# Retention scores from split queries and keys instead of plain fp32 ones

## The chip, the cores and the metric

The kernel runs on one core of a Trainium2 chip. The metric is the time on the device of one execution, in microseconds (us). A core has several engines that run side by side and meet through semaphores: PE (TensorE, the matmuls), DVE (VectorE), ACT (ScalarE), POOL (GpSimd) and SP (SyncE, which issues the weight transfers). PEld is PE's loading of weights, which has rows of its own in the trace.

## The reference

Two transformer blocks on 512 tokens of width 1024: forgetting attention with memory attention, then retention with memory attention, then a third layer of dilated attention, convolution and a gated feed-forward part. The change touches one place, the scores of retention (12 heads, keys of width 64, values of width 128):

```python
qf = rotary(q.reshape(B, S, H, dk).astype(jnp.float32), pos)
kf = rotary(k.reshape(B, S, H, dk).astype(jnp.float32), pos) * (dk ** -0.5)
...
inner = jnp.einsum('bhnd,bhmd->bhnm', qc, kc) * d_inner[None]
o = jnp.einsum('bhnm,bhme->bhne', inner, vc)
...
out = out * lax.rsqrt(jnp.mean(out * out, axis=-1, keepdims=True) + EPS)
```

The reference goes through the 512 tokens in chunks of 128 with a carried state. The kernel computes the same sums without the state, as four 128-row strips of a causal 512 by 512 score matrix per head, multiplied by a table of decays.

## The kernel before

Everything is held with the features on the 128 partitions and the 512 tokens along the free axis. A projection `products(...)` is 8 chunks of 128 input features times three matmuls of 128 by 128 by 512: weights and activations are each a high part in the rounded format fp32r and a low part (the rest), and high times high, high times low and low times high are summed in a PSUM bank (lines 2208 to 2210). One weight block after another goes this way: SP loads it (`wraw`), ACT rounds it (`whi`, line 766), POOL makes the rest (`wlo`, line 611), PE uses it. Each engine runs its own program in the order in which it is written, and all the waits are written out by hand.

Retention is the phase "ret": six turns i = 0 to 5, two heads in each (e = 0 and 1). The two heads of a turn share a tile of 128 partitions: head e has its 64 features in rows 64e to 64e + 63 of `q` and `k`. In a turn PE does, in this order: the projection of the queries (with the two heads' means of the turn before in its middle, lines 2484 and 2485), of the keys, of the first gate, then `ret_scores(i)`, then the projection of the second gate, then `ret_values` and `ret_values_low` (line 2463), which weigh the values.

`ret_scores` writes scores in eight matmuls, one for each head and strip j, with (e, j) in the order (0,0) (1,0) (0,2) (1,1) (0,1) (1,3) (0,3) (1,2). Strip j has 512 - 128j columns, so each head has 512 + 384 + 256 + 128 = 1280 columns. `q` and `k` are plain fp32 tiles here. The matmuls of the two heads use different halves of the rows of the PE array. They write to A0 to A3 and to PV, and PV is shared: strip 2 of head 0 stands in its first half, strip 2 of head 1 in its second. Before the last matmul, (1,2), PE therefore waits on the semaphore `r_half`, which (0,2) raises.

The scores' operands come from `rope` (lines 1710, 1711 and 1714), which runs once for the queries and once for the keys: ACT copies the projection with its 32-row groups swapped into the bank VT (`ret_swap`, line 960, four copies), DVE multiplies the projection by the cosines into `q` or `k`, multiplies VT by the sines, and adds the two. VT serves both, so ACT's swap for the keys waits on `r_roped` until DVE has added the queries. On DVE the queries' rotation of turn i stands behind the end of turn i - 1, that is `ret_low`, `ret_gate` and `ret_out` (lines 1688 to 1702) for the two heads of that turn, which in turn needs the squares and the roots from ACT and the means from PE. Behind the rotation of the keys DVE takes the first gate out of PSUM (`z[0]`, line 1728), then multiplies the scores by the decays (line 1681).

Of the kernel before, what the change touches and what calls it, by code (L numbers as in the profile page):

```python
# [7 lines left out]
F32 = mybir.dt.float32  # L8
F32R = mybir.dt.float32r
BF16 = mybir.dt.bfloat16  # L10
ALU = mybir.AluOpType
# [3 lines left out]
P = 128  # L15
S = 512
# [5 lines left out]
HEADS = 12  # L22
# [6 lines left out]
DK = P // 2  # L29
# [89 lines left out]
def build(nc, t, out):  # L119
# [3 lines left out]
    with ctx:  # L123
        def sb(name, shape, dt=F32, scope=ctx):
            return scope.enter_context(nc.sbuf_tensor(name, shape, dt))
# [4 lines left out]
        def sem(name):  # L130
            return ctx.enter_context(nc.semaphore(name))
# [41 lines left out]
        with ExitStack() as one:  # L173
            Oh = sb("Oh", [P, INNER // P, S], F32R, one)
            Ol = sb("Ol", [P, INNER // P, S], F32R, one)
            Mh = sb("Mh", [P, KC, NMEM], F32R, one)
            Ml = sb("Ml", [P, KC, NMEM], F32R, one)
            with ExitStack() as memory:
                qm_high, qm_low = (sb(f"qm_{part}", [P, S], F32R, memory) for part in ("high", "low"))
            q = sb("q", [P, S], F32, one)  # L180
            k = sb("k", [P, S], F32, one)
            vm_low0 = sb("vm_low0", [P, S], F32R, one)
            with ExitStack() as squared:
                r_high = [sb(f"r_high{e}", [P, S], F32R, squared) for e in range(2)]
# [23 lines left out]
            with ExitStack() as squared:  # L208
                r_low = [sb(f"r_low{e}", [P, S], F32R, squared) for e in range(2)]
# [12 lines left out]
        osq, decayed = (sq2, sq), (probsT, probs)  # L222
        decayed_high = [x[:, HEADS:HEADS + 4, :].rearrange("p c n -> p (c n)")[:, 0:1280] for x in (Oh, Ol)]
        decayed_low = (probs_high[:], turned_low[:])
        maskf, acc2 = sq2[:, 0:P], z[0]

        q_high, k_high, q_low = r_high[0], r_high[1], r_low[1]
# [55 lines left out]
        swapped = VT[:]  # L283
# [65 lines left out]
        r_half = sem("r_half")  # L349
        r_low_made = sem("r_low_made")  # L350
        r_swap, r_roped, r_tanh, r_table = (sem(x) for x in ("r_swap", "r_roped", "r_tanh", "r_table"))
# [20 lines left out]
        def since(eng, s, value):  # L372

            if not isinstance(value, int) or value > 0:
                eng.wait_ge(s, value)
# [99 lines left out]
        def ret_place(e, j):  # L475

            bank, at = ((A[e], 0), (A[2 + e], 0), (PV, 2 * P * e), (A[2 + e], 3 * P))[j]
            return bank[:, at:at + S - j * P]
# [14 lines left out]
        def weighed(r):  # L493

            return 4 * (r // 2) + r % 2 + 1

        def squared(r):

            return weighed(r) + 2

        def split_values(group, j):

            at = slice(4 * group, 4 * group + 4), slice(j * P, (j + 1) * P)
            return Oh[:, at[0], at[1]], Ol[:, at[0], at[1]]
# [914 lines left out]
        def _(dve):  # L1419
            own = Own(dve, dve_own)  # L1420
            tt, ts, stt = dve.tensor_tensor, dve.tensor_scalar, dve.scalar_tensor_tensor
# [5 lines left out]
            def arrived(name, i, b):  # L1427

                dve.wait_ge(w_used, PH[name].n(i, b) + 1)
# [266 lines left out]
            def ret_low(r, e):  # L1696
                dve.wait_ge(r_high_made, squared(r))
                tt(r_low[e][:], osq[e][:], r_high[e][:].bitcast(F32), ALU.subtract).then_inc(r_low_made, 1)
# [5 lines left out]
            def rope(i, b, dst):  # L1704

                ph = PH["ret"]
                arrived("ret", i, b)

                dve.wait_ge(r_swap, i * 2 + (b + 1))
                tt(dst[:], proj[ph.bank(b)][:], rcos[:], ALU.mult).then_inc(evac, 1)  # L1710
                own.mark(tt(swapped, swapped, rsin[:], ALU.mult))
                own.settle()
                dve.wait_ge(evac, ph.g(i, b) + 1)
                tt(dst[:], dst[:], swapped, ALU.add).then_inc(r_roped, 1)

            def ret_turn(i):
                ph = PH["ret"]
                if i:
                    ret_low(i * 2 - 2, 0)
                    ret_low(i * 2 - 1, 1)  # L1720
                    ret_gate(i - 1, 1)
                    ret_out(i * 2 - 2, 0)
                    ret_out(i * 2 - 1, 1)
                rope(i, 0, q)
                rope(i, 1, k)
                arrived("ret", i, 2)
                since(dve, r_table, i * 2 - 1)
                tt(z[0][:], proj[ph.bank(2)][:], rms[:], ALU.mult).then_inc(evac, 1)
                ret_decay(i * 2, 0, i)
                ret_decay(i * 2 + 1, 1, i)  # L1730
                for r in (i * 2, i * 2 + 1):
                    dve.wait_ge(r_high_made, weighed(r))
                    tt(decayed_low[r % 2], decayed[r % 2][:], decayed_high[r % 2].bitcast(F32), ALU.subtract).then_inc(r_low_made, 1)
                ret_gate(i, 0)
                arrived("ret", i, 3)
                since(dve, r_table, i * 2)
                tt(z[1][:], proj[ph.bank(3)][:], rms[:], ALU.mult).then_inc(evac, 1)
# [336 lines left out]
            for c in range(KC - 1):  # L2074
                i, b = divmod(c, 2)
# [102 lines left out]
            for i in range(NT):  # L2178
                for h in range(2):
                    y, at = y_bank[i][h][:], slice(h * S, (h + 1) * S)  # L2180
# [4 lines left out]
                for h in range(2):  # L2185
                    y, at = y_bank[i][h][:], slice(h * S, (h + 1) * S)
# [3 lines left out]
        def _(pe):  # L2190
            mm = pe.matmul
# [254 lines left out]

            def ret_scores(i):

                pe.wait_ge(r_roped, i * 2 + 2)
                since(pe, r_decayed, i * 2)  # L2450
                since(pe, r_out, i * 2)
                for e, j in ((0, 0), (1, 0), (0, 2), (1, 1), (0, 1), (1, 3), (0, 3), (1, 2)):
                    rows = slice(DK * e, DK * e + DK)
                    if (e, j) == (1, 2):
                        pe.wait_ge(r_half, i + 1)
                    ins = mm(ret_place(e, j), k[rows, j * P:(j + 1) * P], q[rows, j * P:S], start=True, stop=True)  # L2456
                    if (e, j) == (0, 2):
                        ins.then_inc(r_half, 1)
                ins.then_inc(r_scores, 1)

            def ret_weigh(e, j, x, y, start=False, stop=False):

                return mm(ret_sum[e][:, j * P:S], x, y[:, TRI[j]:TRI[j] + S - j * P], start=start, stop=stop)  # L2463
# [9 lines left out]

            def ret_values_low(r, e):

                pe.wait_ge(r_low_made, weighed(r))
                for j in range(NT):
                    ins = ret_weigh(e, j, Oh[:, r, j * P:(j + 1) * P], decayed_low[e], stop=(j == NT - 1))
                ins.then_inc(r_pv, 1)

            def ret_mean(r, e):

                pe.wait_ge(r_low_made, squared(r))
                mm(A[2 + e][:], mean_r[:], r_high[e][:], start=True, stop=False)
                mm(A[2 + e][:], mean_r[:], r_low[e][:], start=False, stop=True).then_inc(r_ms, 1)

            def ret_means(i):
                return lambda c: (ret_mean(i * 2, 0), ret_mean(i * 2 + 1, 1)) if c == 4 else None

            def ret_turn(i):  # L2490
                products("ret", i, 0, 0, H, each=ret_means(i - 1) if i else None)
                products("ret", i, 1, 1, H)
                products("ret", i, 2, 2, H)
                pe.wait_ge(v_low, R_VALUE_LOW + HEADS)
                ret_scores(i)
                products("ret", i, 3, 3, H)
                ret_values(i * 2, 0)
                ret_values(i * 2 + 1, 1)
                ret_values_low(i * 2, 0)
                ret_values_low(i * 2 + 1, 1)  # L2500
# [80 lines left out]
            for b in range(HEADS):  # L2581
# [8 lines left out]
                if b == 1:  # L2590
                    pe.wait_ge(rms_ready, 2)
                    for i in range(NT):
                        ins = mm(VT[:, i:i + 1], rms[:, i * P:(i + 1) * P], mean_d[:, 0:1], start=True, stop=True)
# [161 lines left out]
            for b, c in ((0, 0), (0, 1), (0, 2), (1, 0), (1, 1), (1, 2), *((b, c) for c in range(3, KC) for b in range(2))):  # L2755
# [6 lines left out]
                ins = mm(bank[:], wlo[at][:, c, :], Gh[:, c, :], start=False, stop=(c == KC - 1))  # L2762
# [11 lines left out]
            for h in range(2):  # L2774
                y, of = last_out[h][:, 0:HALF], slice(h * HALF, (h + 1) * HALF)
                for c in range(KC):
# [8 lines left out]
                    ins = mm(y, wlo[at][:, c, :], Gh[:, c, of], start=False, stop=(c == KC - 1))  # L2785
# [68 lines left out]
            for c in range(KC):  # L2854
# [5 lines left out]
                ins = mm(A[3][:], wlo[fourth][:, c, :], Hh[:, c, :], start=False, stop=(c == KC - 1))  # L2860
# [38 lines left out]
            def down_part(f, i, h):  # L2899

                s = dn.slot(f // 2 % 2, f % 2)
                y, at, w = y_bank[i][h][:], slice(i * P, (i + 1) * P), slice(4 * h, 4 * h + 4)
                high, low = (x[s][:, w, :].rearrange("p c n -> p (c n)") for x in (whi, wlo))
                mm(y, Fh[:, f, at], high, start=(f == 0), stop=False)  # L2904
                mm(y, Fl[:, f, at], high, start=False, stop=False)  # L2905
                return mm(y, Fh[:, f, at], low, start=False, stop=(f == FC - 1))  # L2906
# [12 lines left out]
            for i, h in tiles:  # L2919
# [8 lines left out]
                for f in range(2):  # L2928
                    ins = down_part(f, i, h)
                    if (i, h) == tiles[-1]:  # L2930
                        ins.then_inc(w_used, 1)
            for f in range(2, FC - 3):
                down_ready(f)
                for i, h in tiles:
                    ins = down_part(f, i, h)
# [71 lines left out]
```

## Time and profile before

| | us |
|---|---|
| median of 3 runs | 1815.93 (1815.48 to 1816.66) |
| the profiled execution, its whole time | 1815.78 |
| its span (first to last instruction) | 1814.1 |
| PE busy | 1806.9 (100% of the span) |
| DVE busy | 942.2 (52%) |
| ACT busy | 773.1 (43%) |
| POOL busy | 789.3 (44%) |

The granted clock of PE was 0.999 of full speed over the span. Rows of the timeline give the start of an instruction and its duration. PE's matmuls are pipelined: a row lasts until its result is complete, and the next one starts before that, so what a matmul costs PE is read from start to start. An fp32 matmul stands in the trace as two rows, each over all of its columns.

### The profile page before, as it was taken

What the parts mean: (1) busy time and instruction counts of PE and PEld (TensorE: products, weight loads), DVE (VectorE), ACT (ScalarE), POOL (GpSimd) and SP (SyncE); (2) the same over time, 40 slices, a digit from 0 to 9 for tenths busy, and PEclk for the clock granted to TensorE, in tenths of its full rate; (3) what the DMA queues carried; (4) which work ended last, traced back from release to release, by engine and by line L of the source; (5) the groups of instructions that cost most, each with busy time, mean ns of one, the idle gap of its engine ahead of it and who ended that gap; (6) DMA issues with size and microseconds to landing.
All of it is one profiled execution on the core that took longest, in us unless ns stands there. A gap on an engine that the chain in (4) does not pass through costs nothing.

```text
span 1814.1 us, 23727 instructions
## 1 busy us (share of the span) xinstructions
PE 1806.9 (100%) x8577; PEld 1506.6 (83%) x8577; DVE 942.2 (52%) x1607; ACT 773.1 (43%) x1240; POOL 789.3 (44%) x380
## 2 busy tenths in 40 slices
PE   9999999999999999999999999999999999999998
PEld 7888888888888888888888888888888888888887
DVE  6246556554111666654259989956333564544202
ACT  5344444443333666643343233257323474444213
POOL 3444444444444333444444543353444454444442
PEclk9999999999999999999999999999999999999999
DMA  5333333333333323332333433322333333333332
GB/s 176 100 93 82 93 82 88 111 87 105 92 93 109 100 81 93 105 93 88 98 93 93 113 88 90 75 82 70 95 102 93 93 94 93 94 103 104 96 101 93
DMA packets 285751, 173.99 MB, mean 96 GB/s; under 512 B 14800, under 2 KB 271208, under 8 KB 285664
## 3 DMA queue, kind: packets, MB, share of 16 engines
q1 hardware_dynamic: 275264, 164.70, 31.7%
q0 software_dynamic: 2496, 8.07, 1.6%
q10 hardware_dynamic: 7904, 0.06, 0.2%
q8 instruction: 55, 0.90, 0.2%
q14 instruction: 32, 0.26, 0.0%
HBM read 170.62 MB, written 2.19 MB: 95 GB/s over the span
## 4 chain that ended last, share of the span: by engine, by line
PE 99%; DVE 0%; ACT 0%; issue 0%; DVEq 0%; ACTq 0%
PE proj L2208 23%; PE proj L2210 23%; PE proj L2209 23%; PE A L2541 1%; PE A L2543 1%; PE A L2542 1%; PE A L2904 1%; PE A L2905 1%; PE A L2906 1%; PE A L2366 1%; PE A L2463 1%; PE PV L2463 1%; PE proj L2543 1%; PE proj L2542 1%; PE proj L2541 1%; PE A L2456 1%
## 5 line engine op out<-in xcount | busy, mean ns | idle before, releaser
L611 POOL TENSOR_TENSOR wlo<-wraw,whi 128x1024 fp32r<-128x1024 f32 (+1 forms) x304 | 723.8, 2385 | 918.4 <-ACT whi L766 914.2
L766 ACT ACTIVATE whi<-wraw 128x1024 fp32r<-128x1024 f32 (+1 forms) x303 | 317.5, 1049 | 613.4 <-DMA wraw<-w_in 168.4
L2208 PE MATMUL proj<-Hh,whi 128*128 128x512 f32 x1424 | 562.5, 395 | 0.0
L2210 PE MATMUL proj<-Hh,wlo 128*128 128x512 f32 x1424 | 555.1, 390 | 0.0
L2209 PE MATMUL proj<-Hl,whi 128*128 128x512 f32 x1424 | 554.7, 390 | 0.0
L2210 PEld LDWEIGHTS proj<-Hh,wlo 128*128 128x128 f32 x1424 | 267.3, 188 | 56.3
L2208 PEld LDWEIGHTS proj<-Hh,whi 128*128 128x128 f32 x1424 | 267.5, 188 | 55.1 <-issue 0.7
L2209 PEld LDWEIGHTS proj<-Hl,whi 128*128 128x128 f32 x1424 | 267.6, 188 | 54.0 <-issue 0.7
L1835 DVE SCALAR_TENSOR_TENSOR A<-cin,dwT,A 128x512 f32<-128x512 f32 x232 | 175.1, 755 | 6.8
L2208 PE MATMUL proj<-Oh,whi 128*128 128x512 f32 x256 | 99.8, 390 | 0.0
L2209 PE MATMUL proj<-Ol,whi 128*128 128x512 f32 x256 | 99.6, 389 | 0.0
L2210 PE MATMUL proj<-Oh,wlo 128*128 128x512 f32 x256 | 99.6, 389 | 0.0
L1748 DVE TENSOR_TENSOR X<-X,proj 128x512 f32 (+1 forms) x16 | 11.0, 687 | 93.9 <-PE proj L2210 93.9
L2144 DVE TENSOR_TENSOR uv<-proj,rms 128x512 f32<-128x512 f32 x21 | 14.5, 692 | 81.2 <-PE proj L2210 81.2
L2210 PEld LDWEIGHTS proj<-Oh,wlo 128*128 128x128 f32 x256 | 48.1, 188 | 9.9
L2209 PEld LDWEIGHTS proj<-Ol,whi 128*128 128x128 f32 x256 | 48.1, 188 | 9.9
L2208 PEld LDWEIGHTS proj<-Oh,whi 128*128 128x128 f32 x256 | 48.1, 188 | 9.8
L2182 DVE TENSOR_TENSOR VT<-VT,gains 128x512 f32<-128x512 f32 x1 | 0.7, 699 | 101.4 <-ACT sq L1408 101.4
L869 ACT ACTIVATE ztanh<-z 128x512 f32<-128x512 f32 x20 | 12.7, 633 | 72.3 <-DVE z L1625 43.2
L2007 DVE TENSOR_TENSOR sq<-proj,rms 128x512 f32<-128x512 f32 x16 | 11.0, 691 | 54.6 <-PE proj L2210 54.3
L1580 DVE RECIPROCAL small<-small 128x4 f32<-128x4 f32 x20 | 3.6, 178 | 67.1 <-ACT probs L840 67.1
L1599 DVE SCALAR_TENSOR_TENSOR ob<-PV,gate 128x512 f32<-128x512 f32 x20 | 13.8, 691 | 47.2 <-PE PV L2389 25.8
(561 smaller groups left out, 3045.2 us busy)
## 6 DMA issues: line engine op xcount, KB each, us to landing
wraw<-w_in SPq DMA_DIRECT2D x68, 512.0 KB, 3.9
wraw<-fox_w_in SPq DMA_DIRECT2D x56, 512.0 KB, 3.8
wraw<-ret_w_in SPq DMA_DIRECT2D x44, 512.0 KB, 3.8
wraw<-w_up SPq DMA_DIRECT2D x44, 512.0 KB, 3.9
wraw<-w_out SPq DMA_DIRECT2D x40, 512.0 KB, 4.1
wraw<-w_down SPq DMA_DIRECT2D x22, 512.0 KB, 3.5
wraw<-w_mem_kv SPq DMA_DIRECT2D x16, 512.0 KB, 3.9
wraw<-conv_pw_w SPq DMA_DIRECT2D x8, 512.0 KB, 4.1
```

Of the source, the lines that this page charges most:

```text
L611: pool.tensor_tensor(wlo[s][:, 0:r, :], wraw[s][:, 0:r, :], whi[s][:, 0:r, :].bitcast(F32), ALU.subtract).then_inc(w_lo, 1)
L766: f(whi[s][:, 0:r, :], wraw[s][:, 0:r, :], ACT.Copy).then_inc(w_hi, 1)
L1835: ins = stt(conv_sum if tap < CONV - 1 else C[:, c, :], cin[:, c, tap:tap + S], dwT[:, c * CONV + tap:c * CONV + tap + 1], conv_sum, ALU.m ...
L2208: mm(dst, whi[s][:, c, :], xh, start=(first and c == 0), stop=False)
L2209: mm(dst, whi[s][:, c, :], xl, start=False, stop=False)
L2210: ins = mm(dst, wlo[s][:, c, :], xh, start=False, stop=(last and c == chunks - 1))
L2366: ins = pe.transpose(A[j][:, (i - j) * P:(i - j + 1) * P], probs[:, FOXAT[i] + j * P:FOXAT[i] + (j + 1) * P], ident[:])
L2456: ins = mm(ret_place(e, j), k[rows, j * P:(j + 1) * P], q[rows, j * P:S], start=True, stop=True)
L2463: return mm(ret_sum[e][:, j * P:S], x, y[:, TRI[j]:TRI[j] + S - j * P], start=start, stop=stop)
L2541: mm(y, Hh[:, x, at], high[:, c, :], start=(x == 0), stop=False)
L2542: mm(y, Hl[:, x, at], high[:, c, :], start=False, stop=False)
L2543: ins = mm(y, Hh[:, x, at], low[:, c, :], start=False, stop=(x == KC - 1))
```

## The change

DVE now makes two tiles from each rotated tile: the rounded high part (written straight from the addition, in format fp32r) and the low part, which is the fp32 sum less the high part. They are put where there is room: the high parts into chunk 15 of `Oh` (queries) and of `Ol` (keys), the low parts into `qm_high` (queries) and `qm_low` (keys). The scores are then key-high times query-high, key-high times query-low and key-low times query-high, each in the eight matmuls of before, accumulated in the same banks. The semaphore `r_low_made`, which counted four steps of a turn, counts seven, and `r_half` is raised five times in a turn.

```diff
+                high, low = roped_high[b], roped_low[b]
+                if b == 0:
+                    own.mark(tt(high, dst[:], swapped, ALU.add))
+                else:
+                    tt(high, dst[:], swapped, ALU.add).then_inc(r_low_made, 1)
                 tt(dst[:], dst[:], swapped, ALU.add).then_inc(r_roped, 1)
+                if b == 0:
+                    own.settle()
+                else:
+                    dve.wait_ge(r_low_made, k_high_count(i))
+                dve.wait_ge(r_roped, i * 2 + (b + 1))
+                tt(low, dst[:], high.bitcast(F32), ALU.subtract).then_inc(r_low_made, 1)
...
-                pe.wait_ge(r_roped, i * 2 + 2)
+                pe.wait_ge(r_low_made, k_high_count(i))
...
-                for e, j in ((0, 0), (1, 0), (0, 2), (1, 1), (0, 1), (1, 3), (0, 3), (1, 2)):
-                    rows = slice(DK * e, DK * e + DK)
-                    if (e, j) == (1, 2):
-                        pe.wait_ge(r_half, i + 1)
-                    ins = mm(ret_place(e, j), k[rows, j * P:(j + 1) * P], q[rows, j * P:S], start=True, stop=True)
-                    if (e, j) == (0, 2):
-                        ins.then_inc(r_half, 1)
+                for n, (x, y) in enumerate(((roped_high[1], roped_high[0]), (roped_high[1], roped_low[0]), (roped_low[1], roped_high[0]))):
+                    if n == 2:
+                        pe.wait_ge(r_low_made, k_low_count(i))
+                    for e, j in ((0, 0), (1, 0), (0, 2), (1, 1), (0, 1), (1, 3), (0, 3), (1, 2)):
+                        rows = slice(DK * e, DK * e + DK)
+                        if (e, j) == (1, 2):
+                            pe.wait_ge(r_half, 5 * i + 2 * n + 1)
+                        if (e, j) == (0, 2) and n:
+                            pe.wait_ge(r_half, 5 * i + 2 * n)
+                        first = n == 0 and (e, j) in ((0, 0), (1, 0), (0, 2), (1, 1), (0, 1))
+                        ins = mm(ret_place(e, j), x[rows, j * P:(j + 1) * P], y[rows, j * P:S], start=first, stop=(n == 2 and (e, j) in ((0, 0), (1, 0), (0, 3), (1, 3), (1, 2))))
+                        if (e, j) == (0, 2) or (e, j) == (1, 2) and n < 2:
+                            ins.then_inc(r_half, 1)
```

PE at the scores of turn 1, before (the names are the banks, then the two operands; what the instruction waits on stands in brackets):

```order
L2456 MATMUL A0<-q,k 128x512 [waits r_decayed,r_out,r_roped,v_low]
L2456 MATMUL A1<-q,k 128x512
L2456 MATMUL PV<-q,k 128x256
L2456 MATMUL A3<-q,k 128x384
L2456 MATMUL A2<-q,k 128x384
L2456 MATMUL A3<-q,k 128x128
L2456 MATMUL A2<-q,k 128x128
L2456 MATMUL PV<-q,k 128x256 [waits r_half]
L2208 MATMUL proj1<-Hh,whi3 128x512 [waits w_lo,evac]
```

The same place in the change, the first product and the start of the second (`Ol` holds the keys' high part, `Oh` and `qm_high` the queries' high and low part):

```order
L2494 MATMUL A0<-Oh,Ol 128x512 [waits r_decayed,r_out,r_low_made,v_low]
L2494 MATMUL A1<-Oh,Ol 128x512
L2494 MATMUL PV<-Oh,Ol 128x256
L2494 MATMUL A3<-Oh,Ol 128x384
L2494 MATMUL A2<-Oh,Ol 128x384
L2494 MATMUL A3<-Oh,Ol 128x128
L2494 MATMUL A2<-Oh,Ol 128x128
L2494 MATMUL PV<-Oh,Ol 128x256 [waits r_half]
L2494 MATMUL A0<-qm_high,Ol 128x512
L2494 MATMUL A1<-qm_high,Ol 128x512
L2494 MATMUL PV<-qm_high,Ol 128x256 [waits r_half]
```

Eight matmuls have become 24, and the waits on `r_half` five instead of one: before each second use of PV, in either direction.

DVE at the rotations of turn 1, before:

```order
L1710 TENSOR_TENSOR q<-proj0,rcos 128x512 [waits r_swap,w_used]
L1711 TENSOR_TENSOR VT<-VT,rsin 128x512
L1714 TENSOR_TENSOR q<-q,VT 128x512 [waits evac,dve_own]
L1710 TENSOR_TENSOR k<-proj1,rcos 128x512 [waits r_swap,w_used]
L1711 TENSOR_TENSOR VT<-VT,rsin 128x512
L1714 TENSOR_TENSOR k<-k,VT 128x512 [waits evac,dve_own]
L1728 TENSOR_TENSOR z0<-proj0,rms 128x512 [waits r_table,w_used]
```

And in the change:

```order
L1731 TENSOR_TENSOR q<-proj0,rcos 128x512 [waits r_swap,w_used]
L1732 TENSOR_TENSOR VT<-VT,rsin 128x512
L1737 TENSOR_TENSOR Oh<-q,VT 128x512 [waits evac,dve_own]
L1740 TENSOR_TENSOR q<-q,VT 128x512
L1746 TENSOR_TENSOR qm_high<-q,Oh 128x512 [waits r_roped,dve_own]
L1731 TENSOR_TENSOR k<-proj1,rcos 128x512 [waits r_swap,w_used]
L1732 TENSOR_TENSOR VT<-VT,rsin 128x512
L1739 TENSOR_TENSOR Ol<-k,VT 128x512 [waits evac,dve_own]
L1740 TENSOR_TENSOR k<-k,VT 128x512
L1746 TENSOR_TENSOR qm_low<-k,Ol 128x512 [waits r_roped,r_low_made]
L1760 TENSOR_TENSOR z0<-proj0,rms 128x512 [waits r_table,w_used]
```

The queries' high part stands ahead of the addition that raises `r_roped`, and its low part behind it; `z0` and the decays behind it stand two more instructions down.

## Rows read from the trace of the kernel before

**Rows 1.** The page: busy time of the engines, and the chain that ended last.

```profile
PE 1806.9 (100%) x8577; PEld 1506.6 (83%) x8577; DVE 942.2 (52%) x1607; ACT 773.1 (43%) x1240; POOL 789.3 (44%) x380
PE 99%; DVE 0%; ACT 0%; issue 0%; DVEq 0%; ACTq 0%
```

**Rows 2.** Busy time by window, from scores to scores (first and last of five).

```profile
592.55:621.63 29.08, 29.08 (x141) 23.93 (x140) 20.10 (x30) 19.41 (x26) 11.08 (x7) 1.00 0.31 91
...
708.87:737.95 29.08, 29.08 (x141) 23.93 (x140) 20.11 (x30) 20.06 (x27) 11.32 (x7) 1.00 0.30 91
```

**Rows 3.** Timeline of PE at the scores of turn 0: start, duration, instruction.

```profile
592.24 0.39 PE L2210 MATMUL proj<-Hh,wlo 128*128 128x512 f32 x1
592.55 1.13 PE L2456 MATMUL A<-q,k 64*128 64x512 f32 x4
593.51 0.38 PE L2456 MATMUL PV<-q,k 64*128 64x256 f32 x1
...
594.70 0.27 PE L2456 MATMUL A<-q,k 64*128 64x128 f32 x1
594.91 0.50 PE L2208 MATMUL proj<-Hh,whi 128*128 128x512 f32 x1
595.25 0.39 PE L2209 MATMUL proj<-Hl,whi 128*128 128x512 f32 x1
```

**Rows 4.** All matmuls of line 2456: counts, durations, forms.

```profile
L2456 PE MATMUL A<-q,k x72: 269/482/693, 592.6 to 740.1; 64*128 64x512 f32 x24, 64*128 64x384 f32 x24, 64*128 64x128 f32 x24
L2456 PE MATMUL PV<-q,k x24: 376/376/378, 593.5 to 740.0; 64*128 64x256 f32 x24
```

**Rows 5.** Timeline of PE at the scores of turn 1.

```profile
621.32 0.39 PE L2210 MATMUL proj<-Hh,wlo 128*128 128x512 f32 x1
621.63 1.13 PE L2456 MATMUL A<-q,k 64*128 64x512 f32 x4
...
623.99 0.50 PE L2208 MATMUL proj<-Hh,whi 128*128 128x512 f32 x1
```

**Rows 6.** Timeline of PE at the values of turn 0, matmuls in fp32r.

```profile
600.50 0.39 PE L2463 MATMUL PV<-Oh 128*128 128x512 f32 x1
600.73 0.39 PE L2463 MATMUL PV<-Oh,Ol 128*128 128x512 f32 x1
...
601.71 0.44 PE L2463 MATMUL A<-Ol,Oh 128*128 128x512 f32 x1
```

**Rows 7.** Timeline at 1408 us, where PE waits for DVE.

```profile
1407.98 0.69 DVE L2077 COPY Y<-proj 128x512 f32<-128x512 f32 x1 [3.93 <-PE proj L2762]
...
1408.72 0.19 PEld L2208 LDWEIGHTS proj<-Gh,whi 128*128 128x128 f32 x1 [0.59 <-DVE Y L2077]
1408.72 0.50 PE L2208 MATMUL proj<-Gh,whi 128*128 128x512 f32 x1 [0.17 <-DVE Y L2077]
...
1409.06 0.39 PE L2209 MATMUL proj<-Gl,whi 128*128 128x512 f32 x1
```

**Rows 8.** Groups by form: fp32r matmuls of 256 columns (busy us, mean ns).

```profile
L2208 PE MATMUL proj<-Mh,whi 128*128 128x256 f32 x64 | 18.1, 282 | 0.0
```

**Rows 9.** Timeline of DVE around the rotations of turn 1.

```profile
614.24 0.69 DVE L1694 TENSOR_TENSOR Ol<-A,Oh 128x512 fp32r<-128x512 f32 x1
614.85 0.68 DVE L1710 TENSOR_TENSOR q<-proj,rcos 128x512 f32<-128x512 f32 x1
615.45 0.69 DVE L1711 TENSOR_TENSOR VT<-VT,rsin 128x512 f32<-128x512 f32 x1
616.17 0.69 DVE L1714 TENSOR_TENSOR q<-q,VT 128x512 f32<-128x512 f32 x1
619.28 0.69 DVE L1710 TENSOR_TENSOR k<-proj,rcos 128x512 f32<-128x512 f32 x1 [2.43 <-ACT VT L960]
...
620.61 0.69 DVE L1714 TENSOR_TENSOR k<-k,VT 128x512 f32<-128x512 f32 x1
621.74 0.69 DVE L1728 TENSOR_TENSOR z<-proj,rms 128x512 f32<-128x512 f32 x1 [0.44 <-PE proj L2210]
```

**Rows 10.** Timeline of ACT ahead of them.

```profile
603.81 0.60 ACT L935 ACTIVATE sq<-PV 128x512 f32<-128x512 f32 x1 [1.31 <-PE PV L2463]
...
616.89 2.29 ACT L960 ACTIVATE VT<-proj 32x512 f32<-32x512 f32 x4 [0.96 <-DVE q L1714]
```

**Rows 11.** Timeline of DVE at the keys' rotation of turn 0.

```profile
591.00 0.69 DVE L1714 TENSOR_TENSOR k<-k,VT 128x512 f32<-128x512 f32 x1
```

More of the change, by code:

```diff
@@ L224, in build @@
         decayed_low = (probs_high[:], turned_low[:])
+        roped_high, roped_low = (Oh[:, HEADS + 3, :], Ol[:, HEADS + 3, :]), (qm_high[:], qm_low[:])
         maskf, acc2 = sq2[:, 0:P], z[0]
@@ L499, in squared, with q_low_count, k_high_count, k_low_count @@
             return weighed(r) + 2
+        def q_low_count(i):
+            return 7 * i + 1
+        def k_high_count(i):
+            return 7 * i + 2
+        def k_low_count(i):
+            return 7 * i + 3
+        def weighed_low(r):
+            return 7 * (r // 2) + r % 2 + 4
+        def squared_low(r):
+            return 7 * (r // 2) + r % 2 + 6
         def split_values(group, j):
@@ L2474, in ret_values_low @@
             def ret_values_low(r, e):
-                pe.wait_ge(r_low_made, weighed(r))
+                pe.wait_ge(r_low_made, weighed_low(r))
                 for j in range(NT):
@@ L2481, in ret_mean @@
             def ret_mean(r, e):
-                pe.wait_ge(r_low_made, squared(r))
+                pe.wait_ge(r_low_made, squared_low(r))
                 mm(A[2 + e][:], mean_r[:], r_high[e][:], start=True, stop=False)
```

## The prediction

> **What bounds the kernel now.** First the page: PE is busy for the whole span, and the chain that ended last is PE at 99% [rows 1]. So the time changes by what PE's own sequence gains or loses, and by any new wait that PE enters. Then the windows by turn: each turn of retention takes 29.08 us and PE is busy in all of it, DVE and ACT in two thirds [rows 2]. The change lies inside these six turns. Last the timeline at the scores, for what they cost, and upstream on DVE and ACT for how late their operands are.
>
> **PE, the scores before.** PE's block of scores runs from 592.55 to the next projection at 594.91, which is 2.36 us [rows 3]; turn 1 has the same, 621.63 to 623.99 [rows 5]. Each fp32 matmul has two rows: 96 rows for 48 matmuls [rows 4]. A projection's 512 columns cost 0.227 us start to start, close to 512 columns at 2.4 GHz (0.213; the granted clock is 1.00 there [rows 2]). Were the two heads' 2560 columns taken one after another at four passes, the block would need 2560 x 4 / 2.4 GHz = 4.27 us; at 2.36 the two row halves must run side by side (1280 x 4 / 2.4 = 2.13). Both ends of the block carry an exposed weight load: the first projection matmul after it is followed 0.34 us later and not 0.227 [rows 3], so the load costs 0.11. That is so before and after the change, since the scores are in 64-row form either way.
>
> **PE, the scores after, without new waits.** An fp32r matmul is one pass. Eight matmuls over 2 x 1280 columns take 600.50 to 601.71 = 1.21 us in 128-row form [rows 6]. If the halves run side by side, one half has three products x 1280 columns, 12 matmuls: 1.5 x 1.21 = 1.81 us; with 0.11 for the first load and 0.09 for leaving the 64-row form (last row at 594.70, a 128-column row of some 0.11 if two passes, next at 594.91 [rows 3]) that is 2.01, or 0.35 less than 2.36. This is the floor.
>
> **PE's waits on itself.** The bank PV is used by both halves, and each use now waits until the other half's is complete: (0,2), (1,2), (0,2), (1,2), (0,2), (1,2), five waits in a row. What is queued behind each on PE is all the rest, the other half's matmuls too, so the free half can't run ahead. In the block before, the one such wait had (0,2) starting at 593.51 and long complete, so its price isn't shown. I bound it. A 256-column fp32r matmul is complete 0.28 us after its start [rows 8]. From a completion to a waiting engine it takes 0.03 us (the projection of 621.32 + 0.39 [rows 5], DVE at 621.74 [rows 9]) to 0.05 us (DVE done at 1408.67, PE's weight load at 1408.72 [rows 7]). Behind a wait the weight load isn't hidden: the matmul after the one at 1408.72 starts 0.34 later, again 0.11 more than 0.227 [rows 7]. So a link costs between 0.28 + 0.03 = 0.31 (load hidden after all) and 0.28 + 0.05 + 0.11 = 0.44. I take 0.43, since the row at 1408.72 is just this case. The block is then 0.11 (load) + 0.23 (until the first (0,2)) + 5 x 0.43 + 0.11 (columns of the last (1,2)) + 0.09 = 2.69 us, which is 0.33 more than before; at 0.31 it would be 2.09. Over six turns: +2.0 us, bounds -1.6 and +2.4 (at 0.44).
>
> The Trainium skill has a rule against this change here ("TensorEngine Tiling (Array Packing)", Gotcha 1: PSUM Pressure): different row tiles can't write one PSUM bank at the same time, and the program must see to it. That is why the waits are there; no row of before shows what happens without them, and the page gives no price.
>
> **DVE, and PE's start.** DVE gets four more instructions of 0.69 us a turn. Back to back without a wait such instructions start 0.60 apart (614.85, 615.45), behind a wait for its own result 0.72 (615.45, 616.17) [rows 9]. In turns 1 to 5 the path to the scores is tight: DVE goes from `ret_out` straight into the queries' rotation (614.24, 614.85), its addition at 616.17 releases ACT's swap for the keys at 616.89, which was idle 0.96 for it [rows 10], the keys' rotation starts behind the swap at 619.28, and the addition is done at 620.61 + 0.69 = 621.30 [rows 9]. PE starts the scores at 621.63 [rows 5], so there were 0.28 us to spare with 0.05 for the release. Now the queries' high part goes ahead of that addition, and the swap and all behind it come 0.60 later; for the keys the high part takes the addition's place, and PE waits for it: done at 621.90, seen at 621.95. PE starts 0.32 us later than before. The path begins at PE's own values (ACT's square at 603.81, released by PE [rows 10]) and the projections between take PE the same time, so the stall comes back in each of turns 1 to 5: 5 x 0.32 = +1.6 us. Bounds: 0 if something upstream absorbs the 0.60, and +3.0 if all of it counts. In turn 0 the addition of the keys starts at 591.00 [rows 11], done at 591.69, and PE is there at 592.55: no stall. The queries' low part runs while ACT swaps (DVE was idle 2.43 [rows 9]): nothing.
>
> **The third product** waits for the keys' low part. The addition follows at 621.81, is done at 622.50, and the low part runs 622.53 to 623.22, seen at 623.27. PE would be ready for it at 621.95 + 0.11 + 0.23 + 3 x 0.43 = 623.58. So it waits for nothing, by 0.3 us; with a link of 0.31 the two meet. This is a second floor: in turns 1 to 5 the block can't end before 623.27 + 0.11 + 0.60 (a third of 1.81) + 0.09 = 624.07, 0.08 later than 623.99, however fast PE is. `z0` behind it on DVE comes 1.5 us later, but nobody needs it soon, and the decays behind wait for the scores anyway; between the scores and the values PE has a whole projection, as before.
>
> **The sum**, against the profiled execution's own time of 1815.78 us: +2.0 +1.6 = +3.6, so 1819.4; the median of the runs is 0.15 above that execution, within their spread, so I leave 1819.4 as the forecast. This is +0.19%. A measurement of this kernel tells some 0.2% (3.6 us) from no change, so the forecast lies at that edge, just within.
>
> **Rivals.** *The self-waits cost little* (links of 0.31 or hidden): then turn 0 gains 0.35 and turns 1 to 5 lose 0.08 each by the keys' low part, +0.05 us, 1815.8; with links of 0.31 exactly, -1.6 + 1.6 = 0 comes out the same. For it: PE can order its work in ways that the rows don't show. Against it: the load at 1408.72 wasn't hidden [rows 7]. *The halves do not run side by side in fp32r* (the slower side): eight matmuls cost 1.21, three products 3.63, with 0.20 at the ends 3.83, which is 1.47 over 2.36; the waits on PV and the third product's are then covered by the other half's matmuls. 6 x 1.47 + 1.6 = +10.4, 1826.2. It decides from the point at which a half's columns can no longer hide behind the other's. For it: before, no fp32r matmul has 64 rows, and fp32's four passes ask less of memory and banks per column. Against it: the fp32 block did overlap [rows 3, 4]. *DVE's 0.60 is absorbed and the waits are cheap*: then the floor of 2.01 counts in all turns, -2.1 us, 1813.7; even this stays under 0.2%.
>
> The Trainium skill ("TensorE: Matmul & The Clock Gate", Part 3: Packing small matmuls) says that matmuls in distinct row groups run concurrently and names no exception for fp32r; this case's fp32 rows agree (2.36 us against 4.27), and no row here shows it for fp32r. By that rule the slow rival falls away and 1819.4 stands.
>
> **How the numbers follow.** Halves overlap and the waits bind, 0.72: of it 0.40 below +3.6 us and 0.32 above, since the forecast is at the edge and the stall may be less than I make it. Cheap waits, 0.12 (same). Halves in series, 0.14 (slower). The gain, 0.02; a part of it might exceed my floor. So faster 0.02, same 0.52, slower 0.46. The range takes the two bounds of the link and the upper part of the stall: 1815.6 (cheap waits) to 1821.8 (+2.4 and +3.0 with something over); the series case is left out, with some 0.04 on the other ends.
>
> **What would show it.** Right: the distance from the first to the next projection matmul at the scores is about 2.7 us, with PE rows of (0,2) and (1,2) some 0.43 apart; from turn to turn it is 29.7 us, not 29.08; the first score row of turn 1 follows the end of the keys' high part by 0.05, and the last projection matmul before it by 0.63 instead of 0.31. The keys' low part ends before the third product starts. Wrong: a block of about 2.0 (waits free), of 3.8 (halves in series), or a first score that doesn't wait for DVE. The forecast fails most easily by the five links: 0.05 us in each is 1.5 us in all.

## The result, and the profile after

| | before | changed |
|---|---|---|
| median, us | 1816.1 (6 runs, 1815.4 to 1816.7) | 1824.2 (6 runs, 1823.6 to 1829.1) |
| profiled execution's span | 1814.1 | 1823.4 |
| ratio | | 1.005 (95% interval 1.0039 to 1.006) |

The change makes the kernel 8.1 us slower. The forecast was 1819.4, within 1815.6 to 1821.8: less than half of the loss. The page of the changed kernel, as [rows 1]:

```profile
PE 1810.2 (99%) x8625; PEld 1509.9 (83%) x8625; DVE 968.0 (53%) x1631; ACT 773.0 (42%) x1240; POOL 789.4 (43%) x380
PE 92%; DVE 4%; ACT 2%; issue 1%; DMA 1%; DVEq 0%; SPq 0%; ACTq 0%
```

DVE, which had 0% of the chain that ended last, now has 4%. That share is no price: 4% of the span is 73 us, and the change lost 8.1. By turn, from first score to first score, as [rows 2] (turn 0 to 1 and turn 4 to 5):

```profile
592.69:623.44 30.75, 29.68 (x149) 24.54 (x149) 25.01 (x34) 19.40 (x26) 11.31 (x7) 1.00 0.30 86
715.04:745.51 30.47, 29.68 (x149) 24.55 (x150) 24.22 (x35) 19.41 (x26) 11.17 (x7) 1.00 0.29 87
```

A turn takes 30.4 to 30.8 us where it took 29.08, and PE is busy in 29.68 of it, so it waits 0.8 to 1.1 us a turn. Where it waits is seen in PE's timeline at the scores of turn 1, as [rows 5] (line 2494 is the scores, 2240 to 2242 the projections):

```profile
622.75 0.39 PE L2242 MATMUL proj<-Hh,wlo 128*128 128x512 f32 x1
623.44 0.50 PE L2494 MATMUL A<-Oh,Ol 64*128 64x512 f32 x2 [0.30 <-issue]
...
624.97 0.38 PE L2494 MATMUL PV<-qm_high,Ol 64*128 64x256 f32 x1
625.82 0.50 PE L2494 MATMUL A<-Oh,qm_low 64*128 64x512 f32 x2 [0.48 <-DVE qm_low L1746]
...
626.80 0.50 PE L2240 MATMUL proj<-Hh,whi 128*128 128x512 f32 x1
```

Two things are new. The first score comes 0.69 us behind the last projection matmul, not 0.31. And between the second product and the third there is a hole: `A<-Oh,qm_low` waits for `DVE qm_low`, the keys' low part. DVE and POOL at that time:

```profile
622.65 0.69 DVE L1739 TENSOR_TENSOR Ol<-k,VT 128x512 fp32r<-128x512 f32 x1
...
622.84 2.37 POOL L632 TENSOR_TENSOR wlo<-wraw,whi 128x1024 fp32r<-128x1024 f32 x1 [2.75 <-ACT whi L787]
...
623.26 0.68 DVE L1740 TENSOR_TENSOR k<-k,VT 128x512 f32<-128x512 f32 x1
...
624.04 1.72 DVE L1746 TENSOR_TENSOR qm_low<-k,Ol 128x512 fp32r<-128x512 f32 x1
```

The low part takes 1.72 us. The two instructions ahead of it have as many elements and take 0.69. They read one operand from PSUM (VT); the low part reads both from SBUF. POOL is in the midst of making low weights, also from SBUF, until 625.21, and the low part is done 0.55 us after that. All instructions of this line, by what they write (min, median and max in ns):

```profile
L1746 DVE TENSOR_TENSOR qm_high<-q,Oh x6: 692/1532/1714, 587.0 to 741.1; 128x512 fp32r<-128x512 f32 x6
L1746 DVE TENSOR_TENSOR qm_low<-k,Ol x6: 1577/1738/2796, 592.5 to 746.1; 128x512 fp32r<-128x512 f32 x6
```

The account over the six turns, by start to start: the block of scores takes 3.67, 3.36, 3.38, 3.63, 3.37 and 3.21 us against 2.36 each, together 6.5 us more; the first score comes 0.37 us later in turns 1 to 5, together 1.9 us. That is 8.3 us, against 8.1 in the medians. The profiled execution of the change was itself slower than its median, 1825.1 us. It is 9.3 us above the profiled one of before, and 0.9 of that lies behind the last block of scores, where the change does nothing.

**The theory**: POOL's making of low weights and a DVE instruction with two SBUF operands exclude each other, and the one that comes second stands until the first is done. A standing instruction shows no wait in the timeline, its row is only longer. **Its rivals**: the low part is slow for another reason (the rounded format, ACT, PE or the transfers), or it is PE's own waits on PV that cost.

### The profile page after: what moved, and what is told of

Its sections match the earlier page's. It is cut to its first block, busy times and chain, and to the rows that moved or that the text cites. A ratio compares the mean times of both kernels' runs of the same rounds, so it can differ in the third digit from the quotient of the medians.

```text
span 1823.4 us, 23859 instructions
## 1 busy us (share of the span) xinstructions
PE 1810.2 (99%) x8625; PEld 1509.9 (83%) x8625; DVE 968.0 (53%) x1631; ACT 773.0 (42%) x1240; POOL 789.4 (43%) x380
## 4 chain that ended last, share of the span: by engine, by line
PE 92%; DVE 4%; ACT 2%; issue 1%; DMA 1%; DVEq 0%; SPq 0%; ACTq 0%
PE proj L2240 21%; PE proj L2242 21%; PE proj L2241 21%; PE A L2579 1%; PE A L2581 1%; PE A L2580 1%; PE A L2944 1%; PE A L2942 1%; PE A L2943 1%; PE A L2398 1%; DVE qm_low L1746 1%; PE PV L2501 1%; PE proj L2579 1%; PE proj L2581 1%; PE proj L2580 1%
```

## Experiments

**1. The keys' low part with one operand from PSUM.** The fp32 sum of the keys stays in VT, which is idle until the next turn:

```diff
-                tt(dst[:], dst[:], swapped, ALU.add).then_inc(r_roped, 1)
+                total = dst[:] if b == 0 else swapped
+                tt(total, dst[:], swapped, ALU.add).then_inc(r_roped, 1)
...
-                tt(low, dst[:], high.bitcast(F32), ALU.subtract).then_inc(r_low_made, 1)
+                tt(low, total, high.bitcast(F32), ALU.subtract).then_inc(r_low_made, 1)
```

> The changed kernel, but the keys' rotated sum is left in the PSUM bank VT, so that the instruction that makes the keys' low part reads one operand from PSUM and one from SBUF instead of two from SBUF. Theory (it stood still because POOL held the SBUF access that a DVE instruction with two SBUF operands needs): the keys' low part takes 0.69 us in every turn instead of 1.58 to 2.80, PE's third product starts without waiting, the block of scores falls from 3.2-3.7 us to about 2.6, and the time from 1824.2 to about 1819 (6 x 0.85 less). Rival (writing rounded format next to a busy PE, ACT or DMA is slow, whatever the operands): it stays at 1.6 us and more, and the time at 1824.

Measured: 1820.9 us (ratio to before 1.0026, 1.0017 to 1.0036), block of scores 2.74 in turn 0 and 2.71 in the others. The low parts' instructions, by what they write:

```profile
L1747 DVE TENSOR_TENSOR qm_high<-q,Oh x6: 691/1485/1662, 586.7 to 736.9; 128x512 fp32r<-128x512 f32 x6
L1747 DVE TENSOR_TENSOR qm_low<-VT,Ol x6: 691/691/691, 592.2 to 741.9; 128x512 fp32r<-128x512 f32 x6
```

The keys' low part takes 0.691 us in all six turns, though POOL is at work as before (592.00 to 594.39 around the one at 592.19); the queries' low part, left as it was, still takes up to 1.66. Format and size are the same in both, so it isn't these. The third product doesn't wait any more. The blocks of scores are 4.3 us shorter in sum; the median fell by 3.3 us and not by the 5 expected. The block was expected at 2.6 us and is 0.1 longer.

This splits the 8.3 us of the change: 4.3 for the meeting with POOL, 2.1 for PE's waits on itself (what the blocks of this run are still over 2.36), 1.9 for the later first score. So the rival of the waits on PV isn't wrong, but it is the smaller part, and about what was forecast.

**2. POOL waits instead.** DVE as in the change:

```diff
                 for b in range(4):
+                    if b == 3:
+                        pool.wait_ge(r_low_made, 7 * i + 3)
                     split("ret", i, b)
```

> The changed kernel with the DVE instructions untouched, but POOL begins the fourth making of low weights of a turn only when the keys' low part is done. Theory (POOL holds what DVE needs): the same DVE instruction with its two SBUF operands takes 0.69 us in every turn, the block of scores about 2.6 us, the time about 1819, and the low weights, two blocks ahead of their use, keep nobody waiting. The queries' low part, which meets POOL's third making, stays at 1.3 to 1.7 us. Rival (the instruction itself is slow there): no change from 1824.

Measured: 1820.4 us (1.0023, 1.0013 to 1.0033), block 2.71 to 2.75. The same view:

```profile
L1748 DVE TENSOR_TENSOR qm_high<-q,Oh x6: 694/1430/1574, 586.9 to 737.2; 128x512 fp32r<-128x512 f32 x6
L1748 DVE TENSOR_TENSOR qm_low<-k,Ol x6: 691/692/693, 592.4 to 742.2; 128x512 fp32r<-128x512 f32 x6
```

POOL's timeline in turn 0 shows it waiting for that instruction:

```profile
593.21 2.38 POOL L632 TENSOR_TENSOR wlo<-wraw,whi 128x1024 fp32r<-128x1024 f32 x1 [3.33 <-DVE qm_low L1748]
```

The very same instruction with two SBUF operands takes 0.69 once POOL stands still. With the first run this settles the cause for this instruction: it took both, the second operand from SBUF and POOL at work.

**3. The queries' sum first.** The sum releases ACT's swap, and the high part is made from it by a copy:

```diff
-                if b == 0:
-                    own.mark(tt(high, dst[:], swapped, ALU.add))
-                else:
+                if b == 1:
                     tt(high, dst[:], swapped, ALU.add).then_inc(r_low_made, 1)
                 tt(dst[:], dst[:], swapped, ALU.add).then_inc(r_roped, 1)
                 if b == 0:
+                    dve.wait_ge(r_roped, i * 2 + 1)
+                    own.mark(dve.tensor_copy(high, dst[:]))
                     own.settle()
```

> The changed kernel, but DVE first adds the queries (which releases ACT's swap for the keys) and makes their high part from that sum by a copy. Theory (the start stall of 0.38 us in turns 1 to 5 is the 0.60 us that the queries' high part puts ahead of ACT's swap): the first score follows the last projection matmul by 0.31 us again and the time falls by 5 x 0.38 = 1.9 us to 1822.3. What may spoil it: copy and low part read SBUF alone, meet POOL's third making, end only at the time at which the swap is done, and hold up the keys' rotation by up to 0.6 us; then the stall stays as it is, with another cause. Rival (the stall has nothing to do with the queries): no change and DVE idle ahead of the keys' rotation as before.

Measured: 1825.5 us (1.0051, 1.0034 to 1.0067): no gain. The stall at the start did go, to 0.46 in turn 1 and 0.31 to 0.32 in turns 2 to 5 behind the last projection matmul. But the blocks of these turns are 3.65 to 3.98 us, where they were 3.21 to 3.63: 1.7 us won at the start and 1.7 lost in the blocks. DVE's keys come earlier, meet POOL earlier in its work and stand longer (timeline of both at turn 1):

```profile
621.79 2.37 POOL L632 TENSOR_TENSOR wlo<-wraw,whi 128x1024 fp32r<-128x1024 f32 x1 [2.76 <-ACT whi L787]
...
622.67 2.04 DVE L1746 TENSOR_TENSOR qm_low<-k,Ol 128x512 fp32r<-128x512 f32 x1
```

The low part begins 0.88 us after POOL's start, where in the change it was 1.20 (622.84, 624.04), and ends 2.92 us after it in both. What sets the end of the block is POOL's end, and that doesn't move with DVE. So what was won was given back at the next wait. In turn 0 of this run DVE came first by 0.08 us, and then it is POOL that stands (2.86 us, not 2.4; timeline of both):

```profile
592.33 0.69 DVE L1746 TENSOR_TENSOR qm_low<-k,Ol 128x512 fp32r<-128x512 f32 x1
...
592.41 2.86 POOL L632 TENSOR_TENSOR wlo<-wraw,whi 128x1024 fp32r<-128x1024 f32 x1 [2.84 <-ACT whi L787]
```

That made the block of turn 0 2.75 us instead of 3.67. The 0.9 us don't show in the median of these four runs, which lie between 1823.9 and 1826.3.

The expectation's warning came true too. The copy that makes the queries' high part reads a single operand, from SBUF, and it stood as well (timeline of POOL and DVE at turn 1, then the copies of all six turns):

```profile
616.64 2.39 POOL L632 TENSOR_TENSOR wlo<-wraw,whi 128x1024 fp32r<-128x1024 f32 x1 [2.55 <-ACT whi L787]
...
617.18 2.13 DVE L1741 CAST Oh<-q 128x512 fp32r<-128x512 f32 x1
```

```profile
L1741 DVE CAST Oh<-q x6: 428/1876/2131, 586.2 to 739.2; 128x512 fp32r<-128x512 f32 x6
```

In turn 0, where POOL began only after it, it took 0.43 us; in the others 1.75 to 2.13. So two operands from SBUF are not the only form that meets POOL: a copy from SBUF to SBUF does too. `CAST Oh<-A`, which reads PSUM, began at 613.80, 0.3 us before POOL's end at 614.09, and took 0.69 like those that met nobody. In turn 1 the stretched copy held up the keys' rotation by 0.4 us, which is why the first score is at 0.46 there.

**4. Both, the edits of 1 and 3.**

> The keys' low part from PSUM and the queries' sum first, both at once. If the two causes are separate, their gains add: about 1819 - 1.9 = 1817, within 0.1% of the kernel before, and what is left over it is the block of scores at 2.5 to 2.6 us against 2.36. If the copy of the queries meets POOL and holds up the keys, it stays at 1819.

Measured: 1818.6 us (1.0014, 1.0005 to 1.0024), where 1817 was expected. First score 0.31 to 0.32 behind the projection and block 2.74 to 2.75 in every turn, 0.1 to 0.2 more than expected. On the change itself the queries' edit was worth nothing in the median; once POOL is out of the way it is worth 2.3 us (run 1 to run 4). What is left is 6 x (2.74 - 2.36) = 2.3 us, against 2.5 measured.

**5. A new order of PE's matmuls on top of 4.** The 24 matmuls now go, as (head, strip, product): (0,2,0) (1,0,0) (0,2,1) (0,0,0) (1,0,1) (0,0,1) (1,2,0) (1,2,1) (0,1,0) (1,1,0) (0,1,1) (1,1,1) (0,3,0) (1,3,0) (0,3,1) (1,3,1) and then, with the keys' low part, (0,2,2) (1,0,2) (0,0,2) (1,1,2) (0,1,2) (1,2,2) (0,3,2) (1,3,2):

```diff
+                    if (e, j, n) == (0, 2, 2):
+                        pe.wait_ge(r_low_made, k_low_count(i))
+                        pe.wait_ge(r_half, 3 * i + 2)
+                    if (e, j, n) in ((1, 2, 0), (1, 2, 2)):
+                        pe.wait_ge(r_half, 3 * i + n + 1)
```

> The kernel of the fourth run (keys' low part from PSUM, queries' sum first) with PE's 24 matmuls in another order: the strips in the shared bank PV are spread out, so that PV changes hands three times with other columns in between, where it was five times back to back, and the products with the keys' low part come last. Theory (what is left over the kernel before is the five links of 0.34 to 0.44 us of PE waiting for itself): the links hide behind other columns, the block of scores falls from 2.74 us to 0.11 + 1.6 for 3840 columns + some 0.2 of gaps + 0.2 at the end = 2.1, under the 2.36 of the kernel before, and the time by 6 x 0.64 = 3.8 us from 1818.6 to about 1814.8, that is 0.07% under the kernel before. Rival (fp32r halves hinder each other, or the 24 pairs can't be issued faster): the block stays at 2.5 and more, the time at 1817 to 1818.

Measured: 1814.9 us (0.9994, 0.9985 to 1.0003), block 2.15 in every turn, a turn 28.86 us against 29.08. PE's timeline at turn 1, first the links in the fourth run, then the first hand-over in this one:

```profile
622.17 0.50 PE L2495 MATMUL A<-Oh,Ol 64*128 64x512 f32 x2
622.50 0.28 PE L2495 MATMUL PV<-Oh,Ol 64*128 64x256 f32 x1
...
622.84 0.38 PE L2495 MATMUL PV<-Oh,Ol 64*128 64x256 f32 x1
...
623.28 0.38 PE L2495 MATMUL PV<-qm_high,Ol 64*128 64x256 f32 x1
...
623.72 0.38 PE L2495 MATMUL PV<-qm_high,Ol 64*128 64x256 f32 x1
```

```profile
621.57 0.39 PE L2496 MATMUL A<-qm_high,Ol 64*128 64x512 f32 x1
621.57 0.37 PE L2496 MATMUL PV<-Oh,Ol 64*128 64x256 f32 x1
621.79 0.28 PE L2496 MATMUL PV<-qm_high,Ol 64*128 64x256 f32 x1
```

In the fourth run PV's users follow each other by 0.34, 0.44 and 0.44 us. Between two of them stand 512 columns of each half, and they take only 0.21 us (512 at 2.4 GHz); everything behind the wait waits too. Now a long matmul of the other half starts together with (1,2), 0.35 us after (0,2,1) was begun at 621.22, and no gap shows. This version's median is 1.1 us under the kernel before, which the interval doesn't tell from no change; the turns' 0.22 us are read from the trace.

**6. The new order alone, on the change.**

> The changed kernel with the new order of PE's matmuls alone; DVE as in the change, so the keys' low part still meets POOL. Theory: what sets the end of the block is the keys' low part, so a faster PE waits longer for it and nearly nothing is gained: third product as late as before, block 3.2 to 3.6 us in turns 1 to 5, time 1823 to 1824 (a gain of 0 to 1 us from the last product, which has fewer links). Rival (PE's own links are what costs): the time falls by 3 us and more, as in the run before.

Measured: 1824.1 us (1.0047, 1.0032 to 1.0063), the same as the change, blocks 3.59 in turn 0 and 3.13 to 3.33 in the others. PE reaches the third product sooner and waits for the keys' low part (timeline, turn 1):

```profile
625.58 0.38 PE L2495 MATMUL PV<-Oh,qm_low 64*128 64x256 f32 x1 [0.76 <-DVE qm_low L1746]
```

It waited 0.48 at this place with the old order. The same new order that was worth 3.7 us in run 5 shortens the blocks by 1.0 us in sum here, within the expected 0 to 1, and nothing of it shows in the median: PE waits for a result that comes no sooner.

**7. DVE's part alone**, PE's scores in plain fp32 as before. The low parts go to other tiles, because in the change they use the memory of `q` and `k`.

```diff
-                pe.wait_ge(r_low_made, k_high_count(i))
+                pe.wait_ge(r_roped, i * 2 + 2)
...
+                    ins = mm(ret_place(e, j), k[rows, j * P:(j + 1) * P], q[rows, j * P:S], start=True, stop=True)
```

> DVE's part of the change alone: the high and low parts are made, at the same places in DVE's order (the low parts into two idle tiles), but PE computes the scores from the plain fp32 tiles as before and waits for the keys' sum. Theory: PE's block is 2.36 us again; the sum of the keys comes 0.6 us behind the high part, so the start stall is 0.38 + 0.6 = 1.0 us in turns 1 to 5, and since nobody on PE waits for the keys' low part, its meeting with POOL costs nothing unless the decays behind it on DVE come late: 1816.1 + 5.0 = 1821. Rival (the low part's delay costs through z0 and the decays too, not only through the third product): 1823 and more.

Measured: 1821.1 us (1.0029, 1.0017 to 1.0041), block 2.35 to 2.36, first score 1.29 behind the projection in turns 1 to 5 (0.32 in turn 0): 5 x 0.97 = 4.9 us. DVE's low part of the keys takes 1.85 us here, though it is written as plain f32 and not in the rounded format, and costs nothing, as PE doesn't wait for it (timeline, turn 1):

```profile
622.58 1.13 PE L2488 MATMUL A<-q,k 64*128 64x512 f32 x4 [0.90 <-issue]
```

```profile
622.58 1.85 DVE L1746 TENSOR_TENSOR ob<-k,Ol 128x512 f32<-128x512 f32 x1
```

## Why the prediction was wrong

**The step that failed** is "The third product": "the low part runs 622.53 to 623.22, seen at 623.27 ... So it waits for nothing, by 0.3 us". Its duration, 0.69 us, was taken from additions that read VT in PSUM [rows 9]. The new instruction reads both operands from SBUF, and it meets POOL: measured 1.58 to 2.80 us. The prediction named each queue on its own engine that the low part could hold up, but never laid POOL's timeline over DVE's. In the kernel before, both were there to see. A DVE instruction with two SBUF operands that met POOL, the gate at 602.53, had taken 1.40 us, twice the 0.68 of the gate at 606.86. POOL's own row at 600.64 is 2.75 us, not 2.36: DVE's `turned_low`, also with two SBUF operands, had begun before it. And POOL's work stood just where the new instruction would come (last row, turn 1):

```profile
599.64 1.49 DVE L1733 TENSOR_TENSOR turned_low<-probs,Ol 128x1280 fp32r<-128x1280 f32 x1
...
600.64 2.75 POOL L611 TENSOR_TENSOR wlo<-wraw,whi 128x1024 fp32r<-128x1024 f32 x1 [1.13 <-ACT whi L766]
...
602.53 1.40 DVE L1702 SCALAR_TENSOR_TENSOR gate<-ztanh,z 128x512 f32<-128x512 f32 x1 [1.40 <-ACT ztanh L952]
...
606.86 0.68 DVE L1702 SCALAR_TENSOR_TENSOR gate<-ztanh,z 128x512 f32<-128x512 f32 x1
...
621.41 2.36 POOL L611 TENSOR_TENSOR wlo<-wraw,whi 128x1024 fp32r<-128x1024 f32 x1 [3.00 <-ACT whi L766]
```

With them the sum can be made: POOL ends at 621.41 + 2.36 = 623.77; the gate above ended 0.54 us after POOL (603.93 against 603.39), so the low part is done at 624.31, not 623.22, and seen at 624.36. PE is ready for it at 623.58 and would wait 0.8 us. That wait hides a part of one link, since what is left behind it is 0.11 + 0.23 + 0.43 + 0.11 + 0.09 = 0.97: the block ends at 625.33 and is 3.38 us, 0.69 more than the forecast's 2.69. Measured in turn 1: 3.36. As an estimate for all six turns that is +4.1, where the change against run 1 shows 4.3. Added to the 3.6 of the forecast it gives 7.7, against 8.1 measured.

The Trainium skill has this rule ("SBUF — State Buffer", section "SBUF: two separate sides"): DVE and GpSimd share one pair of SBUF ports, a DVE instruction with two SBUF inputs needs it against a GpSimd instruction that reads SBUF, and "whichever ... starts first gets the pair for the whole instruction; the other fully blocks". The changed kernel and runs 1 to 3 agree, in both directions (DVE up to 2.80 us in the changed kernel instead of 0.69, POOL 2.86 in run 3 instead of 2.4). The prediction weighed two other rules and left out this one, the one that speaks against the change.

**The first score's stall**: right in cause, 0.32 forecast, 0.37 measured, 1.9 us in all. The rest is the release: the first score's row follows the end of the keys' high part by 0.10 (623.34, 623.44), not by 0.05. Run 4 shows that the stall is the queries' high part ahead of ACT's swap. The bound "+3.0 if all of it counts" was not reached.

**PE's waits on itself**: right. Without DVE's wait the block was forecast at 2.69 and is 2.71 to 2.75 (runs 1, 2 and 4). The five links were taken at 0.43; they measure 0.44. The first reads 0.34 in the rows, because a row behind a wait begins with its weight load (it is 0.38 us long, not 0.28) and the first (0,2) has no wait. Run 5 shows what they cost: 0.6 us a turn. Two small slips in the prediction's sums moved nothing: at 0.44 a link the bound is 6 x 0.38 = +2.3, not +2.4, and the rows that it names give 0.10 for leaving the 64-row form, not 0.09.

**The halves side by side**: right. (1,0) and (0,0) start together and 24 matmuls over 3840 columns a half fit into 2.15 us in run 5, where one after another they would need 3.83 by the prediction's own sum. The rival that had them in series, and that held most of the chance of "slower" beyond the range, was not the one that came: the loss has its sign and about its size (10.4 forecast for it) but another cause. "Slower" had a chance of 0.46 in all, so its coming was held nearly even; the cause that brought it had no chance of its own.

**The second floor**, that the block can't end before the keys' low part and one more product, was the right form. It was put at 624.07 in turn 1; with the low part's real end it is what sets the end of the block in all turns (run 6). The range was too narrow because the low part's duration was given no upper bound: all terms but this one had two ends.

## What to carry to other kernels

A new DVE instruction's duration must be taken from a row with the same kind of operands (SBUF and PSUM are not the same), and its place laid over POOL's timeline, since the two can exclude each other in either direction. Here that held for instructions with two SBUF operands and for a copy from SBUF to SBUF. Leaving one operand in PSUM, or letting POOL wait where its result isn't urgent, takes the meeting away. Where two waits follow each other, an earlier start alone can be worth nothing; and where two halves of the PE array share a bank, put more columns between its users than the hand-over takes.

## What the runs showed of the hardware

A DVE instruction of 512 columns that reads two operands from SBUF takes 0.69 us alone and ended 0.55 us after POOL's end when it met POOL's low weights (1.58 to 2.80 us in the changed kernel). With one operand in PSUM it took 0.69 in all six turns of run 1. A copy from SBUF to SBUF takes 0.43 us alone and 1.75 to 2.13 when it meets POOL (run 3). Whichever comes second stands: POOL took 2.86 us instead of 2.4 in turn 0 of run 3.

Each hand-over of a shared bank between matmuls of two row halves costs 0.44 us from one's columns to the next one's, for 256 columns that take 0.11: 0.28 until the first is complete, 0.06 until the next weight load begins (622.78 to 622.84 in run 4) and 0.10 for that load, which nothing hides. The 512 columns of each half that stood between two users took less than that; with more of them between, the block fell from 2.74 to 2.15 us. Matmuls in fp32r on 64 rows run side by side on the two halves as those in fp32 do (7680 columns in 2.15 us, where 7680 at 2.4 GHz would take 3.2).
